# Hybrid attention and SSD block: dt and the sum of the two directions in the mixing matrix, two products per SSD head, the group norm as a replicated row

## Chip, cores and metric

One core of one Trainium2 chip runs the whole layer. The metric is the device time of one execution in microseconds, as a median of three runs: 1584.28 us (1583.84 to 1584.5).

## What is computed

The layer takes 256 tokens of width 2048. It makes one projection of the normed input, attention in 16 heads, a bidirectional Mamba-2 SSD in 32 heads, an output projection and an MLP. The change touches the SSD alone. Cut to it:

```python
dt = softplus(dt_raw + dt_bias)            # (b, S, 2 directions, 8 groups, 4 heads)
y_fwd = ssd_chunked(xs, dt[:, :, 0], A[0], Bm, Cm)          # chunks of 128 tokens
y_bwd = flip(ssd_chunked(flip(xs), flip(dt[:, :, 1]), A[1], flip(Bm), flip(Cm)))
y = y_fwd + y_bwd + xs * d_skip
y = y.reshape(b, S, SSM_W) * silu(z)
y = rms_norm(y.reshape(b, S, 8, 256), norm_g)   # over the 256 channels of a group
```

With a sequence of two chunks, each head's output is x (256 tokens by 64 channels) multiplied by a 256 x 256 matrix over (source token, target token): C.B of the group, times a decay for each direction, times dt of the source token and direction. The forward direction has nothing in the block "source in chunk 2, target in chunk 1", the backward one nothing in the opposite block.

## The kernel before

The program is written by hand, engine by engine, with semaphores. Every weight matrix is streamed from HBM in chunks of 256 rows by 512 columns (SyncE, `load`). ScalarE rounds each chunk to `w_hi` (L478), VectorE makes `w_lo`, what the rounding left (L776), and TensorE does 24 multiplies of 128x256 (or 12 of 128x512) per chunk with high and low parts (`chunk_by_weights`, `chunk_by_tokens`; all matmuls go through the helper line L1178). Time is counted in slots, one chunk each. ScalarE and VectorE prepare the chunk that is four slots ahead (`high_ahead`, `low_ahead`, LEAD = 4); SyncE loads into eight buffers, and a load waits until TensorE has used the chunk eight back.

SSD work is put in between. A window of 24 slots holds the projections of two groups (x, B, C) and of z. A group's own work starts at `GROUP_SLOT` and goes over some 16 slots, k = 0 to 15, a new group every 12 slots. In each slot an engine does first its part for the chunk, then what the group schedule names, in program order, so what waits in a slot holds up the next chunk's part on that engine. On each engine, by k:

- TensorE: k = 0 transposes x and makes C.B for both chunks (`group_products`, psum banks M0 and M1); k = 5 and 7 the products of two heads each into M0, head by head; k = 10 the sums of squares, in two columns for each half of the tokens; k = 11 spreads the root over all partitions, by a multiply of ones with a diagonal.
- VectorE: k = 1 masks C.B into `cbm` (six blocks of 128 x 128) and scales x by dt for each direction into `xdt_f` and `xdt_b` (`scale_x`, L790); k = 2 to 5 `mix_head` (L799) multiplies a head's six decay blocks by `cbm`; the convolution of the next group in pieces (`CONV_SLOTS`), its SiLU at k = 11; k = 8 the skip and gate; k = 9 the low part of the squares; k = 11 the mean (`group_mean`, L845) and the diagonal (L851); k = 12 the norm; k = 14 the low part of the result.
- ScalarE: the next group's decays for one head at each of `DECAY_SLOTS` (k = 6, 7, 8, 10), four Relu of 128 columns, two Exp of 128 and one of 512; the tanh of the next group's convolution at k = 11; k = 9 the square and its high part; k = 12 copies the spread row out of M1 (L539); k = 13 the high part of the result.
- GpSimd: the power of -0.5 on the two means per token half (`norm_root_of`, L437), and the same for Q and K.
- SyncE: loads the decay rows of a group, replicated over the partitions, at slots 2 and 14 (`decay_loads`), behind a wait until the decays of the group before were made.

Of the kernel before, what the change touches and what calls it, by code (L numbers as in the profile page):

```python
# [28 lines left out]
P = 128  # L29
# [5 lines left out]
EPS = 1e-6  # L35
# [15 lines left out]
DECAY_SLOTS = {6: 0, 7: 1, 8: 2, 10: 3}  # L51
CONV_SLOTS = {3: ((0, 0, 4),), 4: ((1, 0, 2),), 5: ((1, 2, 4),), 6: ((2, 0, 4),), 7: ((3, 0, 4),), 9: ((4, 0, 2),),
              10: ((4, 2, 4),)}
# [26 lines left out]
def build(nc, x, norm_mix_g, w_in, q_norm_g, k_norm_g, rel_bias, conv_w, conv_b, dt_bias, a_log,  # L80
# [17 lines left out]
    with ctx:  # L98
# [71 lines left out]
        xdt_f = place("xdt_f", [P, TT, SEQ], at=at_of(lo2, 2048))  # L170
        norm_diag = place("norm_diag", [P, TT, P], at=at_of(lo2, 1024))
        rnorm = place("rnorm", [P, SEQ], at=at_of(lo2, 1024))

        sq_hi = place("sq_hi", [P, 2, SEQ], f32r, at=cat_base + 32768)
        sq_lo = place("sq_lo", [P, 2, SEQ], f32r, at=at_of(lo2, 2048))
        norm_ms, norm_root = small[:, 32:34], small[:, 34:36]
        gate_n = gate_t
        hi1 = [phase + 4096]
        xdt_b = place("xdt_b", [P, TT, SEQ], at=at_of(hi1, 2048))
# [55 lines left out]
        def sem(name):  # L235
# [20 lines left out]
        args_ready, decays_ready, mix_ready, y_done = (sem(n) for n in (  # L256
            "args_ready", "decays_ready", "mix_ready", "y_done"))
        x_transposed, xtok_ready, cb_done, cb_masked = (sem(n) for n in (
            "x_transposed", "xtok_ready", "cb_done", "cb_masked"))
        gated, gate_squared, norm_summed, ms_ready, root_ready, diag_ready, norm_spread, rn_ready = (sem(n) for n in (  # L260
            "gated", "gate_squared", "norm_summed", "ms_ready", "root_ready", "diag_ready", "norm_spread", "rn_ready"))
        normed, ssd_hi, ssd_lo = sem("normed"), sem("ssd_hi"), sem("ssd_lo")
# [28 lines left out]
        def _(sp):  # L291
# [111 lines left out]
        @block.gpsimd  # L403
        def _(pool):
            pool.memset(ident[:, :], 1.0).then_inc(consts, 1)
            pool.memset(ones[:, :], 1.0).then_inc(consts, 1)
            pool.memset(halfneg[:, :], -0.5).then_inc(consts, 1)
            pool.memset(relw[:, :], 1.0).then_inc(consts, 1)
            pool.memset(one_row[:, :], 1.0).then_inc(consts, 1)
            pool.memset(prefix[:, :, 0:1], 0.0).then_inc(consts, 1)  # L410
            pool.memset(conv_in[:, :, :, 0:2], 0.0).then_inc(consts, 1)
            pool.memset(conv_in[:, :, :, SEQ + 2:SEQ + 4], 0.0).then_inc(consts, 1)
            pool.memset(dtcol[:, 3:4], 1.0).then_inc(consts, 1)
            pool.memset(mask[:, :, :], 1.0).then_inc(consts, 1)
# [19 lines left out]
            def norm_root_of(G):  # L434

                pool.wait_ge(ms_ready, G + 1)
                pool.tensor_tensor(norm_root, norm_ms, halfneg[:, 0:2], ALU.pow).then_inc(root_ready, 1)  # L437

            with pool.Fori(1, 4) as w:
                norm_root_of(2 * (w - 1))  # L440
                norm_root_of(2 * (w - 1) + 1)
            for n in range(2):
                norm_root_of(6 + n)
                qk_root(n)
            with pool.Fori(1, 4) as a:
                qk_root(2 * a)
                qk_root(2 * a + 1)


        @block.scalar  # L450
        def _(act):
# [62 lines left out]

            def conv_tanh_of(G):
# [3 lines left out]
            def next_group(G, i, k):  # L519
# [3 lines left out]
                if k == 11:  # L523
                    conv_tanh_of(G)

            def ssd_slot(s, m, more=True):

                for i, o in enumerate(GROUP_SLOT):
                    G, k = 2 * m + i, s - o
                    if not 0 <= k < 16 or (i == 2 and not more):  # L530
                        continue
                    if k == 9:
# [67 lines left out]
            for s in range(CH - LEAD, WIN):  # L600
# [23 lines left out]
                if s == 19:  # L624
                    conv_tanh_of(0)
                if s == 17:
                    act.wait_ge(m1_free, 1)
                if 17 <= s < 21:
                    decays(0, s - 17)
                next_group(1, 1, s - GROUP_SLOT[2])  # L630
# [86 lines left out]
        def _(dve):  # L717
# [66 lines left out]
            def scale_x(G):  # L784

                dve.wait_ge(x_transposed, G + 1)
                for n, (xdt, H) in enumerate(((xdt_f, 4 * G), (xdt_b, 32 + 4 * G))):
                    dt = tokp[:, 3:5, ds(H, PER_GROUP)].rearrange("p t (h o) -> p t h o", o=1)\
                        .broadcast_to([P, TT, PER_GROUP, 64])
                    ins = tt_(xdt[:, :, :].rearrange("p t (h e) -> p t h e", e=64),  # L790
                              M0.rearrange("p (t h e) -> p t h e", t=TT, e=64), dt, ALU.mult)
                ins.then_inc(xtok_ready, 1)

            def mix_head(G, h):
# [4 lines left out]
                tt_(w[:, :, :], w[:, :, :], cbm[:, :, :], ALU.mult).then_inc(mix_ready, 1)  # L799
# [47 lines left out]
            def group_diag(G):  # L847

                dve.wait_ge(root_ready, G + 1)
                for t in range(TT):  # L850
                    ins = ts_(norm_diag[:, t, :], ident[:, :], norm_root[:, t:t + 1], None, ALU.mult)  # L851
                ins.then_inc(diag_ready, 1)
# [35 lines left out]
            def ssd_slot(s, m, more=True):  # L888

                for i, o in enumerate(GROUP_SLOT):  # L890
# [3 lines left out]
                    if k == 1:  # L894
                        mask_cb(G)
                        scale_x(G)
# [8 lines left out]
                    if k == 11:  # L905
                        group_diag(G)
# [148 lines left out]
            for s in range(CH - LEAD, WIN):  # L1055
# [8 lines left out]
                if s == 21:  # L1064
# [4 lines left out]
                    scale_x(0)  # L1069
# [106 lines left out]
        def _(pe):  # L1176
# [62 lines left out]
            def ssd_slot(s, m, more=True):  # L1239
                for i, o in enumerate(GROUP_SLOT):  # L1240
# [5 lines left out]
                    if k in (5, 7):  # L1246
                        pe.wait_ge(xtok_ready, G + 1)
                        pe.wait_ge(mix_ready, 4 * G + k - 3)
                        for h in (k - 5, k - 4):
                            rows, ch = slice(64 * (h % 2), 64 * (h % 2) + 64), slice(64 * h, 64 * h + 64)  # L1250
                            c0 = SEQ * (h // 2)
                            both, second, first = slice(c0, c0 + SEQ), slice(c0 + P, c0 + SEQ), slice(c0, c0 + P)
                            mm(M0[rows, both], xdt_f[:, 0, ch], mix[h][:, 4:6, :], True, False)
                            mm(M0[rows, both], xdt_b[:, 1, ch], mix[h][:, 0:2, :], False, False)
                            mm(M0[rows, second], xdt_f[:, 1, ch], mix[h][:, 2, :], False, False)
                            mm(M0[rows, first], xdt_b[:, 0, ch], mix[h][:, 3, :], False, True).then_inc(y_done, 1)
                    if k == 10:
# [3 lines left out]
                        for t in range(TT):  # L1261
# [3 lines left out]
                    if k == 11:  # L1265
                        pe.wait_ge(diag_ready, G + 1)
                        pe.wait_ge(ms_ready, G + 1)
                        for t in range(TT):
                            ins = mm(M1[:, P * t:P * (t + 1)], ones_r[:, :].bitcast(f32), norm_diag[:, t, :], True, True)
                        ins.then_inc(norm_spread, 1)  # L1270
# [208 lines left out]
```

## Time and profile before

| | us |
|---|---|
| median of the runs | 1584.28 |
| profiled execution | 1584.14 |
| its span, first to last instruction | 1582.40 |
| TensorE matmul busy | 1554.7 (98%) |
| VectorE busy | 944.8 (60%) |
| ScalarE busy | 733.8 (46%) |
| GpSimd busy | 35.0 (2%) |

Busy is the union of an engine's instructions. TensorE's granted clock is at its full level (0.997 as a mean). The SSD groups stand in the first quarter, from about 93 us to 430 us. Of the sections below, the weight load (PEld) runs beside the multiplies. An f32 multiply is recorded as two entries. "x2" behind a row means two instructions merged; times are starts from the begin of the span, then the length.

### The profile page before, as it was taken

How to read it: one execution, taken by the hardware profiler on the slowest of the kernel's cores; microseconds unless marked ns; L12 is line 12 of the kernel's file. 1: busy time of each engine (PE TensorE's matmuls, PEld its weight loads, DVE VectorE, ACT ScalarE, POOL GpSimd, SP SyncE). 2: the span in 40 equal slices, each digit the busy share in tenths (PEclk: the TensorE clock that was granted, in tenths of full speed). 3: DMA queues.
4: the chain of work that ended last, by engine and by line, in shares of the span. 5: the costliest groups of instructions: out<-in, count | busy, mean ns of one | idle time of the engine just before them, and what ended most of it. 6: DMA issues, size and time to landing. Idle time of an engine off the chain costs nothing.

```text
span 1582.4 us, 25561 instructions
## 1 busy us (share of the span) xinstructions
PE 1554.7 (98%) x9693; PEld 1395.8 (88%) x9693; DVE 944.8 (60%) x1226; ACT 733.8 (46%) x1011; POOL 35.0 (2%) x36
## 2 busy tenths in 40 slices
PE   6999999999999999999999999999999999999998
PEld 6999999998888888888889998899988998889987
DVE  5878787778666666665465554364454455435543
ACT  4476556656354544444443443434433344424431
POOL 0000000000100000000000000000000000000000
PEclk9999999999999999999999999999999999999999
DMA  8776666555566656575656655666555665666564
GB/s 233 227 216 175 184 174 174 172 175 154 161 186 175 180 176 178 175 237 180 195 181 182 185 183 192 193 166 183 190 190 171 186 181 192 191 174 183 186 196 136
DMA packets 186324, 291.50 MB, mean 184 GB/s; under 512 B 13533, under 2 KB 67151, under 8 KB 185984
## 3 DMA queue, kind: packets, MB, share of 16 engines
q1 hardware_dynamic: 183748, 285.92, 60.3%
q10 hardware_dynamic: 2492, 4.36, 0.9%
q8 instruction: 64, 1.05, 0.3%
q14 instruction: 20, 0.16, 0.0%
HBM read 288.04 MB, written 5.34 MB: 185 GB/s over the span
## 4 chain that ended last, share of the span: by engine, by line
PE 95%; DMA 2%; DVE 1%; ACT 1%; issue 0%; DVEq 0%; SPq 0%; ACTq 0%
PE psum L1178 94%; DMA raw<-in_w_in 1%; DVE w_lo L776 1%; DMA x_in<-in_x 1%; PE psum L1288 0%; PE psum L1308 0%; PE psum L1221 0%; DMA decay_rows<-prefix 0%; PE psum L1231 0%; ACT w_hi L478 0%; DVE xg L751 0%; ACT mix L507 0%; ACT squares_act L464 0%; DVE actT_lo L771 0%; SPq L298 0%
## 5 line engine op out<-in xcount | busy, mean ns | idle before, releaser
L776 DVE TENSOR_TENSOR w_lo<-raw,w_hi 128x1024 fp32r<-128x1024 f32 x512 | 611.0, 1221 | 165.4 <-ACT w_hi L478 162.0
L478 ACT ACTIVATE w_hi<-raw 128x1024 fp32r<-128x1024 f32 x512 | 527.8, 1053 | 390.0 <-DMA raw<-in_w_down 166.2
L1178 PE MATMUL psum<-actT_lo,w_hi 128*128 128x256 f32 x1792 | 514.1, 287 | 9.6 <-DVE w_lo L776 9.6
L1178 PE MATMUL psum<-actT_hi,w_hi 128*128 128x256 f32 x1792 | 509.5, 284 | 0.0
L1178 PE MATMUL psum<-actT_hi,w_lo 128*128 128x256 f32 x1792 | 509.4, 284 | 0.0
L1178 PEld LDWEIGHTS psum<-actT_lo,w_hi 128*128 128x128 f32 x1792 | 346.3, 193 | 14.4 <-DVE w_lo L776 9.4
L1178 PEld LDWEIGHTS psum<-actT_hi,w_lo 128*128 128x128 f32 x1792 | 346.3, 193 | 0.2
L1178 PEld LDWEIGHTS psum<-actT_hi,w_hi 128*128 128x128 f32 x1792 | 346.3, 193 | 0.0
L1178 PE MATMUL psum<-w_hi,hid_lo 128*128 128x512 f32 x512 | 199.2, 389 | 0.0
L1178 PE MATMUL psum<-w_lo,hid_hi 128*128 128x512 f32 x512 | 199.2, 389 | 0.0
L1178 PE MATMUL psum<-w_hi,hid_hi 128*128 128x512 f32 x512 | 199.2, 389 | 0.0
L1178 PE MATMUL psum<-w_hi,actT_lo 128*128 128x512 f32 x384 | 153.3, 399 | 0.0
L1178 PE MATMUL psum<-w_lo,actT_hi 128*128 128x512 f32 x384 | 150.0, 391 | 0.0
L1178 PE MATMUL psum<-w_hi,actT_hi 128*128 128x512 f32 x384 | 150.0, 391 | 0.0
L1178 PEld LDWEIGHTS psum<-w_hi,hid_hi 128*128 128x128 f32 x512 | 96.1, 188 | 20.1
L1178 PEld LDWEIGHTS psum<-w_hi,hid_lo 128*128 128x128 f32 x512 | 96.1, 188 | 19.9
L1178 PEld LDWEIGHTS psum<-w_lo,hid_hi 128*128 128x128 f32 x512 | 96.1, 188 | 19.6
L1155 DVE SCALAR_TENSOR_TENSOR acc<-psum,inv_ms,acc 128x512 f32<-128x512 f32 x32 | 22.6, 747 | 146.7 <-PE psum L1178 146.7
L1142 DVE TENSOR_TENSOR relu_sq<-relu_t 128x1024 f32<-128x1024 f32 x16 | 19.6, 1226 | 147.1 <-ACT relu_t L696 147.1
L1178 PE MATMUL psum<-w_hi,cat_lo 128*128 128x512 f32 x256 | 100.8, 394 | 0.0
L1178 PE MATMUL psum<-w_hi,cat_hi 128*128 128x512 f32 x256 | 99.8, 390 | 0.0
L1178 PE MATMUL psum<-w_lo,cat_hi 128*128 128x512 f32 x256 | 99.8, 390 | 0.0
(192 smaller groups left out, 1277.7 us busy)
## 6 DMA issues: line engine op xcount, KB each, us to landing
raw<-in_w_in SPq DMA_DIRECT2D x128, 512.0 KB
raw<-in_w_up SPq DMA_DIRECT2D x128, 512.0 KB
raw<-in_w_down SPq DMA_DIRECT2D x128, 512.0 KB
raw<-in_w_out SPq DMA_DIRECT2D x64, 512.0 KB
raw<-in_w_in SPq DMA_DIRECT2D x64, 256.0 KB
raw<-in_w_in SPq DMA_DIRECT2D x128, 128.0 KB
decay<-decay_rows SPq DMA_DIRECT2D x16, 512.0 KB, 5.5
rel_tiles<-rel_rows ACTq DMA_DIRECT2D x1, 3072.0 KB, 19.8
```

What stands on the lines that cost most here:

```text
L478: act.activation(w_hi[j][:, :, :], raw[j][:, :, :], ACT.Copy).then_inc(hi_ready, 1)
L776: tt_(w_lo[j][:, :, :], raw[j][:, :, :], w_hi[j][:, :, :].bitcast(f32), ALU.subtract).then_inc(lo_dve, 1)
L1142: tt_(relu_sq[:, :, :], relu_t[:, :, :], relu_t[:, :, :], ALU.mult).then_inc(relu_squared, 1)
L1155: stt_(acc[:, n, t, :], bank_pair(n)[:, t, :], inv_ms[:, 2, t:t + 1], acc[:, n, t, :], ALU.mult, ALU.add).then_inc(down_added, 1)
L1178: return pe.matmul(o, lhsT, rhs, start=first, stop=last, **kw)
```

## The change

The mixing matrix gets dt and the sum of both directions: `mix_head` multiplies each of a head's six blocks by dt of its source token and direction (a scalar per partition) and by `cbm` in one operation (four instructions for the blocks 0-1, 2, 3, 4-5), and then adds block 2 to block 1 and block 3 to block 4, after a wait for its own products. With it a head has one 256-wide matrix row of blocks for each chunk of source tokens, so TensorE does two products a head (256 columns each), in the order chunk 1 of both heads, chunk 2 of both heads. `scale_x` goes; ScalarE copies x from M0 to `xtok` at k = 1 (`copy_x`).

The norm's sum of squares is made by four multiplies of ones with the squares, 256 columns, so each partition holds the whole row. VectorE takes the mean of it (256 columns, `group_mean`), ScalarE makes Ln and Exp with scale -0.5, and VectorE one Newton step in three dependent instructions ahead of the norm. The diagonal, its multiplies, the copy out of M1 and GpSimd's power for the SSD are gone.

In the schedule, the fourth head's decays go from k = 10 to 12, two pieces of the convolution from 9 and 10 to 8 and 9 (behind the own work of the group in that slot), the tanh from k = 11 to 10, and the decay loads from slots 2 and 14 to 5 and 17.

```diff
-DECAY_SLOTS = {6: 0, 7: 1, 8: 2, 10: 3}
-CONV_SLOTS = {3: ((0, 0, 4),), 4: ((1, 0, 2),), 5: ((1, 2, 4),), 6: ((2, 0, 4),), 7: ((3, 0, 4),), 9: ((4, 0, 2),),
-              10: ((4, 2, 4),)}
+DECAY_SLOTS = {6: 0, 7: 1, 8: 2, 12: 3}
+CONV_SLOTS = {3: ((0, 0, 4),), 4: ((1, 0, 2),), 5: ((1, 2, 4),), 6: ((2, 0, 4),), 7: ((3, 0, 4),), 8: ((4, 0, 2),),
+              9: ((4, 2, 4),)}
...
-                if s == 2 and m is not None:
+                if s == 5 and m is not None:
                     sp.wait_ge(decays_ready, 8 * m + 4)
                     load_decay(2 * m + 1)
-                if s == 14 and m is not None and w is not None:
+                if s == 17 and m is not None and w is not None:
...
+            def copy_x(G):
+                act.wait_ge(x_transposed, G + 1)
+                act.activation(xtok[:, :, :], M0.rearrange("p (t s) -> p t s", t=2), ACT.Copy).then_inc(xtok_ready, 1)
...
-                if k == 11:
+                if k == 10:
                     conv_tanh_of(G)
...
-                    if k == 12:
-                        act.wait_ge(norm_spread, G + 1)
-                        act.activation(rnorm[:, :], M1[:, 0:SEQ], ACT.Copy).then_inc(m1_free, 1)
+                    if k == 11:
+                        act.wait_ge(m1_free, G + 2)
+                        act.activation(log_ms[:, :], mean_sq[:, :], ACT.Ln).then_inc(ln_ready, 1)
+                        act.wait_ge(ln_ready, G + 1)
+                        act.activation(rnorm[:, :], log_ms[:, :], ACT.Exp, scale=-0.5).then_inc(rn_ready, 1)
...
             def mix_head(G, h):
-                tt_(w[:, :, :], w[:, :, :], cbm[:, :, :], ALU.mult).then_inc(mix_ready, 1)
+                for k0, k1, src, col in ((0, 2, 4, 32 + H), (2, 3, 4, H), (3, 4, 3, 32 + H), (4, 6, 3, H)):
+                    ins = stt_(w[:, k0:k1, :], w[:, k0:k1, :], tokp[:, src, ds(col, 1)], cbm[:, k0:k1, :],
+                               ALU.mult, ALU.mult)
+                ins.then_inc(scaled, 1)
+                dve.wait_ge(scaled, H + 1)
+                tt_(w[:, 1:5:3, :], w[:, 1:5:3, :], w[:, 2:4, :], ALU.add).then_inc(mix_ready, 1)
...
             def group_mean(G):
-                ts_(norm_ms, M1[:, 0:2 * TT:2], 1.0 / (4 * 256), EPS, ALU.mult, ALU.add).then_inc(ms_ready, 1)
+                ts_(mean_sq[:, :], M1[:, 0:SEQ], 1.0 / (4 * 256), EPS, ALU.mult, ALU.add).then_inc(m1_free, 1)
             def group_norm(G):
+                dve.wait_ge(rn_ready, G + 1)
+                stt_(newton[:, :], rnorm[:, :], -0.5, rnorm[:, :], ALU.mult, ALU.mult).then_inc(newton_step, 1)
+                dve.wait_ge(newton_step, 3 * G + 1)
+                tt_(newton[:, :], newton[:, :], mean_sq[:, :], ALU.mult).then_inc(newton_step, 1)
+                dve.wait_ge(newton_step, 3 * G + 2)
+                stt_(rnorm[:, :], newton[:, :], 1.5, rnorm[:, :], ALU.add, ALU.mult).then_inc(newton_step, 1)
+                dve.wait_ge(newton_step, 3 * G + 3)
...
-                            mm(M0[rows, both], xdt_f[:, 0, ch], mix[h][:, 4:6, :], True, False)
-                            mm(M0[rows, both], xdt_b[:, 1, ch], mix[h][:, 0:2, :], False, False)
-                            mm(M0[rows, second], xdt_f[:, 1, ch], mix[h][:, 2, :], False, False)
-                            mm(M0[rows, first], xdt_b[:, 0, ch], mix[h][:, 3, :], False, True).then_inc(y_done, 1)
+                        for t in range(TT):
+                            for h in (k - 5, k - 4):
+                                ins = mm(M0[64 * (h % 2):64 * (h % 2) + 64, SEQ * (h // 2):SEQ * (h // 2 + 1)],
+                                         xtok[:, t, 64 * h:64 * h + 64], mix[h][:, 4 - 4 * t:6 - 4 * t, :],
+                                         t == 0, t == TT - 1)
...
-                        for t in range(TT):
-                            for n, (sq, c) in enumerate(((sq_lo, 0), (sq_lo, 1), (sq_hi, 0), (sq_hi, 1))):
-                                ins = mm(M1[:, 2 * t:2 * t + 2], sq[:, c, P * t:P * t + P], ones_r[:, 0:2], n == 0, n == 3)
+                        for c in range(2):
+                            mm(M1[:, 0:SEQ], ones_r[:, :], sq_lo[:, c, :], c == 0, False)
+                            ins = mm(M1[:, 0:SEQ], ones_r[:, :], sq_hi[:, c, :], False, c == 1)
```

## Rows read from the trace of the kernel before

**Rows 1.** The page: TensorE's busy time, and shares of the chain by engine.

```profile
PE 1554.7 (98%) x9693; PEld 1395.8 (88%) x9693; DVE 944.8 (60%) x1226; ACT 733.8 (46%) x1011; POOL 35.0 (2%) x36
...
PE 95%; DMA 2%; DVE 1%; ACT 1%; issue 0%; DVEq 0%; SPq 0%; ACTq 0%
```

**Rows 2.** Windows: length, busy of PE, PEld, DVE, ACT, POOL; clock, DMA share, GB/s.

```profile
220.04:262.32 42.28, 42.28 (x343) 40.46 (x342) 32.72 (x51) 26.38 (x49) 1.64 (x1) 1.00 0.60 172
...
346.88:388.00 41.12, 41.12 (x235) 34.62 (x234) 33.73 (x52) 25.35 (x48) 1.61 (x1) 1.00 0.53 154
```

**Rows 3.** Timeline of TensorE across a pair of heads (start, length, what).

```profile
235.03 0.28 PE L1178 MATMUL psum<-actT_hi,w_lo 128*128 128x256 f32 x1
235.15 0.28 PE L1178 MATMUL psum<-actT_hi,w_hi 128*128 128x256 f32 x1
235.36 0.43 PE L1178 MATMUL psum<-mix,xdt_f 128*64 128x256 f32 x1
...
236.28 0.43 PE L1178 MATMUL psum<-mix,xdt_f 128*64 128x256 f32 x2
...
236.55 0.38 PE L1178 MATMUL psum<-mix,xdt_f 128*64 128x256 f32 x1
236.60 0.27 PE L1178 MATMUL psum<-mix,xdt_b 128*64 128x128 f32 x1
...
237.95 0.28 PE L1178 MATMUL psum<-actT_hi,w_lo 128*128 128x256 f32 x1
```

**Rows 4.** Timeline of TensorE at the norm's two steps of a group.

```profile
254.78 0.28 PE L1178 MATMUL psum<-ones_r,sq_lo 128*128 128x2 f32 x2
...
255.79 0.28 PE L1178 MATMUL psum<-actT_hi,w_lo 128*128 128x256 f32 x1
...
258.55 0.61 PE L1178 MATMUL psum<-norm_diag,ones_r 128*128 128x128 f32 x4
...
259.11 0.28 PE L1178 MATMUL psum<-actT_hi,w_lo 128*128 128x256 f32 x1
```

**Rows 5.** VectorE: timeline (first three), groups by shape (busy us, mean ns, idle before).

```profile
233.25 0.95 DVE L799 TENSOR_TENSOR mix<-mix,cbm 128x768 f32<-128x768 f32 x1
234.12 0.88 DVE L816 SCALAR_TENSOR_TENSOR conv<-conv_in,parA,conv 128x256 f32<-128x256 f32 x2
...
255.77 0.16 DVE L845 TENSOR_SCALAR small<-psum 128x2 f32<-128x2 f32 x1 [2.01 <-PE psum L1178]
...
L816 DVE SCALAR_TENSOR_TENSOR conv<-conv_in,parA,conv 128x256 f32<-128x256 f32 x96 | 40.7, 478 | 0.0
L799 DVE TENSOR_TENSOR mix<-mix,cbm 128x768 f32<-128x768 f32 x32 | 30.4, 951 | 0.0
L1155 DVE SCALAR_TENSOR_TENSOR acc<-psum,inv_ms,acc 128x512 f32<-128x512 f32 x32 | 22.6, 747 | 146.7 <-PE psum L1178 146.7
...
L944 DVE TENSOR_TENSOR qkT_lo<-psum,qkT_hi 128x256 fp32r<-128x256 f32 x16 | 6.6, 415 | 0.0
```

**Rows 6.** ScalarE: groups by shape (first two), then its timeline.

```profile
L539 ACT ACTIVATE rnorm<-psum 128x256 f32<-128x256 f32 x8 | 3.1, 385 | 22.1 <-PE psum L1178 22.1
...
L454 ACT ACT_TABLE_LOAD x1 | 1.3, 1283 | 1.3 <-PEq L1466 1.3
...
251.61 1.27 ACT L507 ACTIVATE mix<-decay,tokn 128x128 f32<-128x128 f32 x4
...
253.88 1.05 ACT L478 ACTIVATE w_hi<-raw 128x1024 fp32r<-128x1024 f32 x1
```

**Rows 7.** Group 0: SyncE's wait (total, times, longest), timelines of VectorE and TensorE.

```profile
SPq L326 <- ACT mix L513: 8.5, 1, 8.5
...
105.66 1.22 DVE L776 TENSOR_TENSOR w_lo<-raw,w_hi 128x1024 fp32r<-128x1024 f32 x1 [2.63 <-ACT w_hi L478]
...
125.22 0.69 DVE L903 TENSOR_TENSOR sq_lo<-gate_sq,sq_hi 128x512 fp32r<-128x512 f32 x1 [0.23 <-ACT sq_hi L536]
...
127.94 0.28 PE L1178 MATMUL psum<-ones_r,sq_lo 128*128 128x2 f32 x2
```

More of the change, by code:

```diff
@@ L169, in build @@
         gate_sq = place("gate_sq", [P, 2, SEQ], at=at_of(lo2, 2048))
-        xdt_f = place("xdt_f", [P, TT, SEQ], at=at_of(lo2, 2048))
-        norm_diag = place("norm_diag", [P, TT, P], at=at_of(lo2, 1024))
+        xtok = place("xtok", [P, TT, SEQ], at=at_of(lo2, 2048))
+        mean_sq = place("mean_sq", [P, SEQ], at=at_of(lo2, 1024))
+        log_ms = place("log_ms", [P, SEQ], at=at_of(lo2, 1024))
         rnorm = place("rnorm", [P, SEQ], at=at_of(lo2, 1024))
+        newton = place("newton", [P, SEQ], at=at_of(lo2, 1024))
         sq_hi = place("sq_hi", [P, 2, SEQ], f32r, at=cat_base + 32768)
-        sq_lo = place("sq_lo", [P, 2, SEQ], f32r, at=at_of(lo2, 2048))
-        norm_ms, norm_root = small[:, 32:34], small[:, 34:36]
+        sq_lo = place("sq_lo", [P, 2, SEQ], f32r, at=lo2[0] - 3072)
         gate_n = gate_t
         hi1 = [phase + 4096]
-        xdt_b = place("xdt_b", [P, TT, SEQ], at=at_of(hi1, 2048))
         mask = place("mask", [P, 5, P], at=at_of(hi1, 2560))
@@ L255, in build @@
         decay_in = sem("decay_in")
-        args_ready, decays_ready, mix_ready, y_done = (sem(n) for n in (
-            "args_ready", "decays_ready", "mix_ready", "y_done"))
+        args_ready, decays_ready, scaled, mix_ready, y_done = (sem(n) for n in (
+            "args_ready", "decays_ready", "scaled", "mix_ready", "y_done"))
         x_transposed, xtok_ready, cb_done, cb_masked = (sem(n) for n in (
             "x_transposed", "xtok_ready", "cb_done", "cb_masked"))
-        gated, gate_squared, norm_summed, ms_ready, root_ready, diag_ready, norm_spread, rn_ready = (sem(n) for n in (
-            "gated", "gate_squared", "norm_summed", "ms_ready", "root_ready", "diag_ready", "norm_spread", "rn_ready"))
-        normed, ssd_hi, ssd_lo = sem("normed"), sem("ssd_hi"), sem("ssd_lo")
+        gated, gate_squared, norm_summed, ln_ready, rn_ready, newton_step, normed, ssd_hi, ssd_lo = (sem(n) for n in (
+            "gated", "gate_squared", "norm_summed", "ln_ready", "rn_ready", "newton_step", "normed", "ssd_hi", "ssd_lo"))
         z_tanh, z_ready = sem("z_tanh"), sem("z_ready")
@@ L432, in qk_root, with att_window @@
                 pool.tensor_tensor(qk_s[:, 2, :], qk_s[:, 1, :], halfneg[:, :], ALU.pow).then_inc(qk_rs, 1)
[L434 to L445, printed above, removed]
+            def att_window(a):
                 qk_root(2 * a)
                 qk_root(2 * a + 1)
+            att_window(0)
+            with pool.Fori(1, 4) as a:
+                att_window(a)
         @block.scalar
@@ L531, in ssd_slot @@
                         continue
+                    if k == 1:
+                        copy_x(G)
                     if k == 9:
@@ L623, in _ @@
                     xbc_copy(1, 1, 0)
-                if s == 19:
+                if s == 18:
                     conv_tanh_of(0)
@@ L629, in _ @@
                     decays(0, s - 17)
+                if s == 21:
+                    copy_x(0)
                 next_group(1, 1, s - GROUP_SLOT[2])
@@ L781, in low_ahead @@
                 low(U0 + n, j)
[L784 to L792, printed above, removed]
             def mix_head(G, h):
@@ L895, in ssd_slot @@
                         mask_cb(G)
-                        scale_x(G)
                     if 2 <= k < 6:
@@ L904, in ssd_slot @@
                             .then_inc(sq_low, 1)
-                    if k == 11:
-                        group_diag(G)
                     if k == 12:
@@ L1068, in _ @@
                     mask_cb(0)
-                    scale_x(0)
                 if s > 21:
@@ L1248, in ssd_slot @@
                         pe.wait_ge(mix_ready, 4 * G + k - 3)
[L1249 to L1252, printed above, removed]
-                            mm(M0[rows, both], xdt_f[:, 0, ch], mix[h][:, 4:6, :], True, False)
-                            mm(M0[rows, both], xdt_b[:, 1, ch], mix[h][:, 0:2, :], False, False)
-                            mm(M0[rows, second], xdt_f[:, 1, ch], mix[h][:, 2, :], False, False)
-                            mm(M0[rows, first], xdt_b[:, 0, ch], mix[h][:, 3, :], False, True).then_inc(y_done, 1)
+                        for t in range(TT):
[3 more added lines that the diff above has]
+                                         t == 0, t == TT - 1)
+                                if t == TT - 1:
+                                    ins.then_inc(y_done, 1)
                     if k == 10:
@@ L1260, in ssd_slot @@
                         pe.wait_ge(cb_masked, G + 1)
-                        for t in range(TT):
-                            for n, (sq, c) in enumerate(((sq_lo, 0), (sq_lo, 1), (sq_hi, 0), (sq_hi, 1))):
-                                ins = mm(M1[:, 2 * t:2 * t + 2], sq[:, c, P * t:P * t + P], ones_r[:, 0:2], n == 0, n == 3)
+                        for c in range(2):
+                            mm(M1[:, 0:SEQ], ones_r[:, :], sq_lo[:, c, :], c == 0, False)
+                            ins = mm(M1[:, 0:SEQ], ones_r[:, :], sq_hi[:, c, :], False, c == 1)
                         ins.then_inc(norm_summed, 1)
[L1265 to L1270, printed above, removed]
             def att_slot(s, g):
```

4 lines of the change are left out of this document (removed).

## Prediction

> **What bounds the kernel now.** I read the busy line and the chain of waits first, then sums by stretch, then engine timelines of one SSD group, then the costs by shape. TensorE is busy 98% of the span and carries 95% of the chain [rows 1]. In the stretches of one SSD group (12 chunks of 24 projection multiplies, 42.28 us) it is busy all 42.28 us; VectorE is busy 32.72 us (some 1.1 more in even groups, where the SiLU of z falls, 1024 columns), ScalarE 26.38 [rows 2]. So until another engine becomes the pacer, TensorE time taken out of a group comes out of the total one for one. There are 8 groups; number 6 runs at 41.12 us [rows 2].
>
> **TensorE, the products.** A projection multiply starts 0.12 us after the last (235.03, 235.15), so two steps are 0.24. Across the products of one pair of heads, from the last multiply before (235.15) to the second after (237.95), it takes 2.80: net 2.56 us a pair [rows 3]. Each f32 product is recorded as two passes; head one's first starts at 235.36. Head two's first pass starts at 236.28 and its second at 236.55, while head one's last is still to start at 236.60 [rows 3]: the two heads write different halves of the partitions and do run at once. Backwards from 237.95: head two has four passes of 256 columns and four of 128. I take 0.27 us for the first (236.28 to 236.55), three at 0.215 and four at half of that, the rate at which one pass would use 512 clocks; they end at 237.62, so the exit is 0.33, and the entry (235.15 to 235.36) 0.21.
> After the change a pair is two products a head, all of 256 columns, the heads in turn: four passes a head. If they overlap wholly: 0.21 + 0.27 + 3 x 0.215 + 0.33 - 0.24 = 1.22, a gain of 1.34 a pair, 21.5 us for 16. If nothing overlaps, eight passes: 0.21 + 0.27 + 7 x 0.215 + 0.33 - 0.24 = 2.08, a gain of 0.48, 7.7 in all. I take overlap, because head two was seen to start four passes ahead of head one's end.
> The Trainium skill ("TensorE: Matmul & The Clock Gate", Part 3 on packing small matmuls) says that multiplies keep program order in start and end. The row above shows a later one started first, so it does not hold here to the letter. By that rule head two would trail by one pass, 0.215 us a pair, and TensorE's gain would be 18 us instead of 21.5.
>
> **TensorE, the norm.** The eight two-column multiplies take 254.78 to 255.79 less one step: 0.89 us; the spreading of the diagonal 258.55 to 259.11 less one step: 0.44 [rows 4]. Four multiplies of 256 columns in the rounded type take their place, shape and type of the projections: 0.48. Gain 0.85 a group, 6.8 in all.
> TensorE alone: 2 x 1.34 + 0.85 = 3.53 a group, 28.3 us in all, a group of 38.75 us (group 6: 37.6). Without overlap 1.81 a group, 14.5 in all, a group of 40.47.
>
> **VectorE.** An instruction occupies it for its duration less 0.09 (the mix of 0.95 at 233.25, the next at 234.12 [rows 5]). By shape [rows 5]: scalar-tensor-tensor of 256 columns 0.48, of 512 0.75, so 128 columns about 0.34; tensor-tensor of 256 columns 0.415, of 768 0.95, so 512 columns 0.68; a w_lo of 1024 columns 1.22 [rows 7]. What I give for other lengths is from these slopes, about 1.05 us per 1000 columns. A dependent instruction waits for the full duration plus some 0.03.
> Per head: now 0.86. After: 2 x 0.39 + 2 x 0.25, the last one's 0.09 back, 0.03, and the sum 0.33: 1.75; +0.9, or 3.6 a group. Rows of before bound the four shapes tightly (0.25 to 0.39 each for the short ones: up to +1.1 a group). The scaling of x goes: 2 x 0.59 = -1.2. The mean becomes 256 columns: +0.3. The diagonal goes: -0.4. The three dependent Newton steps: 0.51 + 0.45 + 0.51 = +1.5. Sum +3.8 a group. As occupancies a group without the z part is then: 12 w_lo x 1.13 = 13.6, four heads 7.0, convolution 7.7 (4 x 0.33 and 16 x 0.40), mask 0.9, silu 1.1, gate 1.5, low parts 0.6 + 0.8, mean 0.35, Newton and norm 2.1: 35.7; with z 36.8. Against 38.75 that fits only if VectorE hardly waits.
>
> **ScalarE.** Added: the copy of x (512 columns, 0.55), and Ln and Exp of 256 columns (0.39 each [rows 6]) for the copy of the row. The trace has a single table load, 1.28 us [rows 6], for Square, Copy, Relu, Exp and Tanh together. Whether Ln shares these tables it doesn't show: nothing, or a load out and one back in every group, 2.6 us. I take two loads: every function that is used now has already had its place under the one load, and Ln is the only new one. The Trainium skill ("ScalarE: Activation LUTs", on table sets) lists Exp with Tanh in one set and Ln in another.
> The loads fall between the mean and the row's reciprocal root. The POOL work and its wait go (0.6 us idle, off the path).
>
> **The loop VectorE - ScalarE - VectorE.** Let VectorE's mean start at 0. ScalarE has just done the conv's tanh and splits chunk 15 until 0.95; VectorE's w_lo of it ends at 2.1 (0.6 idle), silu at 3.2. ScalarE: load, Ln, load, Exp (1.28 + 0.39 + 1.28 + 0.39): row at 4.3, the split of chunk 16 at 5.3 (1.05 less 0.09 [rows 6]). VectorE idles 2.1 until it; w_lo, Newton, norm: 8.5. ScalarE makes a head's decays (2.27, from 251.61 to 253.88 [rows 6]) and splits chunk 17 at 8.5; w_lo 9.7, mask 10.6. The next split comes after cat_hi, the copy of x and, in odd groups, the conv's copy: at 11.0 or 11.9, again 0.4 or 1.3 idle. From there VectorE has all it needs to the end of its list: 38.9, with z (even) 40.0, with the conv's copy (odd) 39.8. Today 2.0 us of idle stand at that mean alone [rows 5], which is the room that this uses up.
> So a group is about 39.9 us, paced by this loop, TensorE waiting 1.15 us each for the low part of the squares (it needs it after the chunk of slot 10). Groups 1 to 5: 5.75. Group 6, where TensorE would run at 37.6: 2.4. Group 7 has no next group to prepare and its VectorE has room: 0.
> Group 0: today the squares' low part ends at 125.8 and TensorE wants it at 127.94 [rows 7]. With 3.6 for the heads and 0.8 for the two convolution pieces moved ahead of it, it would be at 130.2, TensorE (2.7 earlier) at 125.3. But x is not scaled (-1.2), and the 8.5 us wait of SyncE for the decays [rows 7], behind which the weight loads stood and VectorE idle for 2.63 us, goes as the load is issued three slots later: about 125.9 to 126.4. I put 0.6 us on it. The later decay loads still land well ahead (5 slots of some 3 us before use): nothing.
> Sum: 28.3 - 5.75 - 2.4 - 0.6 = 19.5 us. The profiled execution took 1584.14 (span 1582.40 and 1.7 around it), the median of the runs is 1584.28. Forecast 1564.8.
>
> **Rivals.**
> (a) The products don't overlap. For: the new order has not run, and overlap was seen only at the seam of two heads. Against: that seam. TensorE then gains 14.5; at 40.47 it paces itself, but for 0.7 in group 6: 1570.5.
> (b) Ln costs no loads, or they stand beside other work. The loop is 2.6 shorter, 37.4, and TensorE stays the only bound: 28.3 - 0.6: 1556.6.
> (c) A table switch costs more than its row. The one load has 1.3 us of idle before it [rows 6]; if that were part of it, 2.6 each, the loop is 42.5: 5 x 3.75 + 4.9 + 0.6 = 24.2 lost, 1580.2. The Trainium skill ("ScalarE: Activation LUTs", on what a table load costs) adds a drain and gives 2.66 us a switch: by it 1581. Against: the row puts that idle time to another engine's sequencer, at the program's start; there was then nothing to drain, so it weighs little either way.
> (d) Slower: the same loop on ScalarE, between Ln and Exp, becomes longer than the gain. With c the group, TensorE's gain is gone at 0.6 + 5(c - 38.75) + (c - 37.6) = 28.3, c = 43.2, a switch of 2.9 us. At 3.5 us: c = 44.3, 1591.
> (e) The sum of the directions is one wait longer, or the short shapes cost as the long ones: +1 to +2 us a group on the loop, 1571 to 1576.
>
> **Numbers.** Forecast (1561 to 1569) 0.5; (b) 0.18; (a) and (e) 0.23; (c) 0.05; (d) 0.03; nothing of it 0.01. The range 1556 to 1574 leaves out about 0.15. 0.2% is 3.2 us, what a measurement here can tell from no change: faster (below 1581.1) 0.94, same 0.03, slower 0.03.
>
> **What would show it.** TensorE in turn: pairs' starts overlapping, 1.5 us from the last multiply before to the second after (2.3 if not). Multiplies of ones with the squares at 0.12. Two loads of 1.28 us a group, VectorE idle about 2 us before w_lo of chunk 16. Groups of about 39.9 us with a TensorE wait of some 1 us for sq_lo. VectorE busy about 36.5 to 37.6 a group. The forecast is wrong if there is no TensorE wait in the groups (then b), or if the loads are not there or longer.

## The result, and the profile after

| | before | after |
|---|---|---|
| median, us (lowest to highest) | 1584.06 (1583.76 to 1584.5) | 1574.49 (1573.56 to 1575.52) |
| profiled execution, its span | 1584.14, 1582.40 | 1575.52, 1573.80 |

The ratio is 0.994, with an interval of 0.9922 to 0.9957: faster by 9.6 us, where 19.5 were forecast, and 0.5 us outside the range. The page of the changed kernel, its busy line and its chain by engine, against [rows 1]:

```profile
PE 1532.7 (97%) x9501; PEld 1375.0 (87%) x9501; DVE 969.9 (62%) x1346; ACT 761.7 (48%) x1043; POOL 22.9 (1%) x28
...
PE 79%; DVE 9%; issue 5%; ACT 4%; DMA 2%; DVEq 1%; ACTq 0%; SPq 0%
```

TensorE has lost 16 points of the chain: 8 to VectorE, 3 to ScalarE, as forecast, and 5 to "issue", in which an engine waits for nothing that the profile shows. The share alone says little: most of these 74 us are pauses of less than 0.3 us or some 1 us long between dependent instructions, and e1 below, 9 us faster, still has 79% and 4%. What needs an explanation is the one long piece among them, 3.73 us. The windows of groups 0 to 5 of the changed kernel, each from the transposes of a group to those of the next (columns as in [rows 2], which has 42.28 for each):

```profile
93.99:132.90 38.91, 38.91 (x317) 37.40 (x317) 34.15 (x61) 28.00 (x50) 0.00 (x0) 1.00 0.66 186
...
132.90:172.94 40.04, 38.96 (x319) 37.34 (x317) 35.76 (x66) 29.76 (x53) 0.00 (x0) 1.00 0.62 185
172.94:217.21 44.27, 40.57 (x318) 38.45 (x317) 37.02 (x67) 28.97 (x52) 0.00 (x0) 0.96 0.59 167
217.21:257.26 40.05, 38.97 (x319) 37.34 (x317) 35.75 (x66) 29.77 (x53) 0.00 (x0) 1.00 0.61 184
257.26:302.17 44.91, 40.52 (x318) 38.83 (x317) 37.64 (x68) 30.43 (x55) 0.00 (x0) 0.96 0.58 164
302.17:340.88 38.71, 38.71 (x318) 37.28 (x317) 35.14 (x66) 28.56 (x50) 0.00 (x0) 1.00 0.63 190
```

Groups 1 and 3 are the forecast's 39.9. Groups 2 and 4 are 4.4 and 5.0 longer, at a lower clock, and the last row gives 1.2 back. VectorE's timeline where group 2 and group 4 go wrong (the bracket is the idle before an instruction and what ended it), and the piece of the chain of waits at the first of them (start, length, what; DVEq is VectorE's sequencer, L1087 the line of its loop over the SSD windows):

```profile
191.51 1.23 DVE L778 TENSOR_TENSOR w_lo<-raw,w_hi 128x1024 fp32r<-128x1024 f32 x1 [3.86 <-issue]
...
274.99 1.23 DVE L778 TENSOR_TENSOR w_lo<-raw,w_hi 128x1024 fp32r<-128x1024 f32 x1 [3.02 <-issue]
```

```profile
186.95 0.70 DVE conv L809 x2
187.66 3.73 issue
191.38 0.08 DVEq L1087
```

The trace has the loop's COMPARE_BRANCH at 186.88 and at 271.20; the sequencer's next instruction follows 4.50 and 3.67 us later, and before the change 0.33 and 0.31 us later. Two things went up with it: VectorE's recorded instructions in one turn of the loop (two SSD groups), from 251 and 255 to 320, and the packets of the instruction queue q14, from 20 to 32 in the whole execution. From 95 to 345 us, first before and then after the change:

```profile
q14 instruction: 4, 0.03, 0.0%
...
q14 instruction: 14, 0.11, 0.2%
```

The packets' times point at the jumps. The kernel before has none from 149 to 373 us, over both of its jumps; the changed kernel has them at 189.34, 192.39 and 196.46 behind the first jump, at 273.03, 275.59 and 280.14 behind the second, and six more elsewhere in that stretch. So the theory: the body had become too long to be still at hand at the jump back, and VectorE waits until it is fetched. The Trainium skill ("Runtime: NRT & Kernel Launch", on instruction fetch mechanics) has this mechanism: a taken branch whose target isn't in the window at hand forces a fetch by DMA. Its window of 512 instructions for engines other than TensorE is larger than any turn recorded here, so its size alone doesn't tell when the fetch begins. The section also says that the window is two blocks of 256, of which the next is fetched while the current one runs; how much of it lies behind the jump, no run here shows.

TensorE then waits. Its table of waits (for what, us in total, times, the longest), all those of over 2 us:

```profile
PE psum L1311 <- DMA rowsB<-in_k_norm_g: 10.7, 1, 10.7
PE psum L1171 <- DVE w_lo L778: 9.6, 4, 2.7
PE psum L1171 <- DVE sq_lo L899: 7.9, 5, 2.6
PE psum L1171 <- DVE mix L796: 4.4, 2, 2.6
```

The first two rows are of before too. The wait for sq_lo was forecast at some 8.8 in all; the one for the mix is the late VectorE. And something follows the longest ones. TensorE in group 2, at the products after such a wait:

```profile
198.34 1.60 PE L1171 MATMUL psum<-mix,xtok 128*64 128x256 f32 x8 [2.60 <-DVE mix L796]
...
200.47 0.41 PE L1171 MATMUL psum<-actT_hi,w_hi 128*128 128x256 f32 x1
200.68 0.41 PE L1171 MATMUL psum<-actT_lo,w_hi 128*128 128x256 f32 x1
```

and the windows from there, and from the end of the wait of 2.62 us for sq_lo in group 4:

```profile
198.34:201.90 3.56, 3.56 (x17) 2.61 (x18) 3.56 (x6) 1.83 (x7) 0.00 (x0) 0.56 0.18 50
294.35:297.80 3.45, 3.45 (x16) 3.45 (x17) 2.85 (x5) 2.66 (x3) 0.00 (x0) 0.51 0.17 50
```

The granted clock is at the lower of its two levels (1.2 instead of 2.4 GHz) for 3.4 us, multiplies follow each other by 0.21 instead of 0.12 us, and each time some 1.7 us more are lost (half of the 3.4). Group 2 by these rows: 2.60 and 1.7 = 4.3 beyond its usual wait; group 4: 1.76 + 2.62 + 1.7 - 1.1 = 5.0.

### The profile page after: what moved, and what is told of

Its sections match the earlier page's. It is cut to its first block, busy times and chain, and to the rows that moved or that the text cites. A ratio compares the mean times of both kernels' runs of the same rounds, so it can differ in the third digit from the quotient of the medians.

```text
span 1573.8 us, 25410 instructions
## 1 busy us (share of the span) xinstructions
PE 1532.7 (97%) x9501; PEld 1375.0 (87%) x9501; DVE 969.9 (62%) x1346; ACT 761.7 (48%) x1043; POOL 22.9 (1%) x28
## 4 chain that ended last, share of the span: by engine, by line
PE 79%; DVE 9%; issue 5%; ACT 4%; DMA 2%; DVEq 1%; ACTq 0%; SPq 0%
PE psum L1171 77%; DVE w_lo L778 2%; DVE mix L792 2%; DVE conv L813 2%; ACT w_hi L470 1%; DMA raw<-in_w_in 1%; DMA x_in<-in_x 1%; PE psum L1275 0%; PE psum L1295 0%; PE psum L1214 0%; ACT mix L499 0%; ACT L537 0%; ACT conv_t L513 0%; DVE gate_t L832 0%; DMA decay_rows<-prefix 0%
```

## The experiments

Fourteen kernels were run, each timed beside the kernel before on the same chip. VectorE's "jump" is the time from the COMPARE_BRANCH to its sequencer's next instruction, first and second turn.

| kernel | median, us | ratio (interval) | a group, us | turn; jump |
|---|---|---|---|---|
| changed | 1574.49 | 0.994 (0.9922 to 0.9957) | 40.04, 44.27, 40.05, 44.91, 38.71 | 320; 4.50, 3.67 |
| e1: loop written out | 1565.54 | 0.9879 (0.9863 to 0.9896) | 40.03, 40.24 | none |
| e2: no Ln | 1563.91 | 0.9866 (0.985 to 0.9883) | 38.71, 44.44, 38.71, 42.31 | 320; 6.10, 4.91 |
| e3: both | 1557.38 | 0.9829 (0.9812 to 0.9845) | 38.71 | none |
| e4: e3, head by head | 1556.77 | 0.9824 (0.9807 to 0.984) | 38.73 | none |
| e5: new mix, old norm | 1575.11 | 0.9945 (0.9928 to 0.9962) | 39.56, 43.23, 39.56, 46.81 | 310; 5.37, 6.63 |
| e6: e5, loop written out | 1564.39 | 0.9878 (0.9861 to 0.9894) | 39.56 | none |
| e7: old mix, new norm | 1582.01 | 0.998 (0.997 to 0.9989) | 41.43 | 264; 0.33, 0.31 |
| e8: before, 72 more a turn | 1583.99 | 1.0 (0.999 to 1.0009) | 42.28 | 326, 322; 2.87, 3.08 |
| e9: before, loop written out | 1584.2 | 1.0004 (0.9994 to 1.0013) | 42.28 | none |
| e10: e1, tanh at slot 19 | 1566.44 | 0.989 (0.9873 to 0.9906) | 40.05, 40.26 | none |
| e11: e10, no Newton step | 1564.45 | 0.9878 (0.9861 to 0.9894) | 39.65, 39.89 | none |
| e12: before, 24 more a turn | 1585.21 (one run) | | 42.28 | 278, 275; 0.33, 0.31 |
| e13: e1, decays at k = 14 | 1566.21 | 0.9885 (0.9868 to 0.9901) | 40.03, 40.24 | none |
| e14: e13, no Newton step | 1557.65 | 0.9827 (0.9811 to 0.9844) | 38.71, 38.82 | none |

**The fetch.** e1 writes VectorE's loop out; e9 does the same to the kernel before.

```diff
-            with dve.Fori(1, 4) as w:
+            for w in range(1, 4):
```

> The changed kernel, but VectorE's loop over the three SSD windows is written out (no jump back; the other engines keep their loops). Theory A: the 3.86 and 3.02 us of idle after the loop's two jumps on VectorE (187.66 and 271.97 us in the changed kernel's trace), which nothing in the profile explains, is the fetch of the loop's code; in its wake TensorE stalls and its clock falls. Then both stretches without work on VectorE are gone, groups 2 and 4 take 40.0 us as groups 1 and 3 do (44.3 and 44.9 now), group 5 goes from 38.7 to about 40, TensorE's granted clock stays full in the SSD part: 7 to 8 us less, about 1567. Theory B: the idle belongs to something else at that place (a weight load that is late, a wait): 1574 to 1575 as now.

Two windows of e1, groups 1 and 2:

```profile
132.39:172.42 40.03, 38.96 (x318) 37.34 (x317) 35.73 (x66) 29.76 (x53) 0.00 (x0) 1.00 0.63 184
172.42:212.66 40.24, 38.96 (x318) 37.33 (x317) 36.86 (x67) 28.95 (x52) 0.00 (x0) 1.00 0.66 183
```

The long groups are gone, the low clock in the SSD part with them, q14 is at 22 packets, and the time is 1565.5: 1.5 us below what was expected of this run, and 0.7 above the 1564.8 of the prediction.

> The kernel before, with VectorE's loop over the SSD windows written out. Control for the written-out loop alone. Theory (the loss of the change is the fetch after VectorE's jump, and the turn of the loop before, 251 to 255 recorded instructions, is short enough not to need it): no fetch to take away, so 1584 us within 1.5. Rival (writing the loop out saves something of its own, register arithmetic or branches, and the 9 us it gave on the changed kernel are not the fetch): 1575 to 1580.

Nothing changed: writing the loop out gives nothing where there is no fetch. e8 and e12 lengthen the turn of the kernel before (`dve.sem_inc(filler, 1)`, three or one in each slot).

> The kernel before, its VectorE loop over the SSD windows made longer by 72 semaphore increments that nothing waits for (from some 255 recorded instructions a turn to some 327, the changed kernel has 320). Theory A, the loop's length against the instruction buffer: idle of 3 to 5 us without a releaser on VectorE behind each of the two jumps and instruction packets on queue 14 there, neither of which the kernel before has. VectorE has some 8 us of idle a group to take it up, so the time changes little: 1584 to 1588. Theory B (the idle comes from what the new instructions do, not from their number): no such idle; 1584 to 1585.

> The kernel before with one more semaphore instruction in each slot of VectorE's loop, 24 a turn, so about 275 to 279 recorded instructions a turn (264 jumped without delay, 310 with 5.4 us, 322 to 326 with 2.9 us until VectorE's next sequencer instruction). One look, to narrow where the fetch starts. If the limit is some 256 plus what the engine has already passed on, the delay after the jump is there; if it lies nearer to 310, the next sequencer instruction follows within 0.4 us. The time stays at 1584 in both cases, since the loop's VectorE has 2.7 us of other work behind the jump.

With 322 to 326 instructions q14 rises to 31 packets and the jump takes 2.9 us, though nothing of the change is in this kernel; with 278 it takes 0.33. q14 has 11 packets from 150 to 350 us in e8, as in the changed kernel, and none in e12 and e7. So the fetch begins between 278 and 310 recorded instructions a turn, and more instructions alone make it. Whether the length of the turn decides, or where the jump falls in the whole stream, was not separated: the first jump is the 409th to 434th recorded VectorE instruction in the runs without a fetch, the 476th to 486th in those with one. But e8 lost no time. Its VectorE around the jump at 183.81:

```profile
183.12 1.22 DVE L777 TENSOR_TENSOR w_lo<-raw,w_hi 128x1024 fp32r<-128x1024 f32 x1
184.25 0.95 DVE L800 TENSOR_TENSOR mix<-mix,cbm 128x768 f32<-128x768 f32 x1
185.12 1.38 DVE L813 TENSOR_SCALAR conv<-conv_in,parA,parB 128x256 f32<-128x256 f32 x4
186.81 1.23 DVE L777 TENSOR_TENSOR w_lo<-raw,w_hi 128x1024 fp32r<-128x1024 f32 x1 [0.30 <-issue]
```

Its sequencer had passed 2.7 us of work to the engine ahead of the gap, so VectorE stood for 0.30 us only; the changed kernel had 0.8 us there, and its groups had no slack for the rest.

**One half of the change alone.** e5 has the new mixing and products and keeps the old norm, e7 the reverse; e6 is e5 with the loop written out.

> The kernel before with only the first half of the change: dt and the sum of the directions in mix_head, two products a head with the heads in turn, x copied by ScalarE, and the schedule's moves. The norm is the old one. TensorE should save 2.68 us a group (39.6), VectorE's loop has neither the table loads nor the Newton steps and is below that, the idle after the jumps is absorbed in part. If so 20 to 21 us less than before, 1563 to 1565. If VectorE's extra 3.6 us a group are alone too much: about 40 to 41 us a group, 1568 to 1574.

> The mixing half of the change alone on the kernel before, with VectorE's SSD windows written out. If code fetch after the jump took its gain (1575.1 with the loop, groups of 43.2 and 46.8 us among four of 39.6), all groups from 1 to 5 are 39.6 and the time is 1563 to 1565. If it was something else, 1573 to 1576.

> The other half alone: the changed kernel with the old scaling of x, the old mix_head and the four products a head. TensorE saves 0.85 us a group (41.4); the loop of VectorE and ScalarE with its two table loads is some 37.5 and doesn't pace it: 6 to 7 us less than before, about 1577.5. If the table loads or the Newton steps are late for TensorE by themselves: no gain, 1580 to 1585.

e5 missed its expectation for the reason that e1 names: a turn of 310. e6 has TensorE busy in all of its 39.56 us a group; that it is as fast as e1 (1564.39 against 1565.54) says what the new norm is worth beside the new mix: nothing. e7's group, 41.43, is the 42.28 - 0.85 of the forecast, to the hundredth. At the start of the second MLP quarter its profiled execution was 6.1 us ahead of the one before, as expected, but 1.5 us at the end: its waits for w_lo at the ends of MLP quarters are up to 4.0 us long instead of 2.7, in a part that the change doesn't touch, and the granted clock is at its lower level for 6.8 us around the last of them (0.50 from 1393.62 to 1400.45). Its ten runs go from 1578.19 to 1583.91, so much of this is the spread of executions; why their median is only 2.9 us below that of before stays open.

**The table loads.** e2, e3 and e4 make a Copy in the place of Ln, so their root is not the norm's.

```diff
-                        act.activation(log_ms[:, :], mean_sq[:, :], ACT.Ln).then_inc(ln_ready, 1)
+                        act.activation(log_ms[:, :], mean_sq[:, :], ACT.Copy).then_inc(ln_ready, 1)
```

> The changed kernel with Copy in place of Ln, so that ScalarE needs no other table (the root's value is then another one). Theory A: the 16 table loads (20.5 us on ScalarE) stand in the loop VectorE - ScalarE - VectorE that paces a group; without them the loop is some 2.5 us shorter, about 37.5, below TensorE's 38.8. Groups 1 and 3 at 38.8, groups 2 and 4 still with the idle after the jump but absorbed in part (about 41), group 6 about 38: 10 to 12 us less, about 1563. Theory B: the loads lie beside other work and VectorE's own length paces the group: no more than 2 us less, 1572 to 1574.

> The changed kernel with VectorE's SSD windows written out and Copy in place of Ln (so no table loads; the root's value is another one). If the table loads and the jump's fetch are all that keeps the TensorE saving back, every group from 1 to 5 takes 38.7 to 38.85 us and group 6 about 37.5, with no TensorE wait after group 0: 1557 (8 us less than with the windows written out alone). If VectorE's own length still paces: 39 us or more a group, 1560 to 1563.

e3's windows show TensorE without a wait, at 38.72 us; the forecast had 38.75 for TensorE alone:

```profile
131.50:170.22 38.72, 38.72 (x319) 37.29 (x318) 36.30 (x69) 28.02 (x52) 0.00 (x0) 1.00 0.62 189
```

**The order of the heads.** e4 is e3 with the loops over t and h exchanged: both products of one head, then both of the other.

> As e3_unroll_noloads, but the four products of a pair head by head (both products of head one, then both of head two). TensorE paces here, so its cost shows in full. If the gain of the alternation is that two heads' passes run at once, and head by head only part of them can: between nothing and full overlap lost, which is up to 0.86 us a pair, 1.7 a group: groups of 39.2 to 40.5 us, 1561 to 1571. The passes before the change suggest that the second head can still start some passes early, so I expect the lower half of it, about 1564. If the order doesn't matter: groups of 38.8, 1557.

Missed: no difference. TensorE at one pair of heads in the changed kernel, and then in e4 (eight recorded passes merged in a row):

```profile
188.51 0.28 PE L1171 MATMUL psum<-actT_hi,w_hi 128*128 128x256 f32 x1
188.71 1.08 PE L1171 MATMUL psum<-mix,xtok 128*64 128x256 f32 x8
189.73 0.39 PE L1171 MATMUL psum<-actT_lo,w_hi 128*128 128x256 f32 x1
189.95 0.28 PE L1171 MATMUL psum<-actT_hi,w_lo 128*128 128x256 f32 x1
```

```profile
148.41 0.28 PE L1171 MATMUL psum<-actT_hi,w_hi 128*128 128x256 f32 x1
148.62 1.09 PE L1171 MATMUL psum<-mix,xtok 128*64 128x256 f32 x8
149.64 0.39 PE L1171 MATMUL psum<-actT_lo,w_hi 128*128 128x256 f32 x1
```

Eight passes in 1.08 us in either order: the engine runs two heads at once when four passes of one stand ahead of the other's as well. In the changed kernel the passes start two at a time, 0.01 us apart (188.71 and 188.72, then 188.98 and 188.99), and so they do in e4. The gain of the products comes from two f32 products a head instead of four, not from the turns.

**The start.** e10 puts the tanh of group 0 back from slot 18 to slot 19 of the first window; in the changed kernel its first transposes come 1.3 us later than before.

> The changed kernel with VectorE's loop written out and the tanh of group 0 put back to slot 19 of the first window. Theory for the start: the tanh in slot 18 stands ahead of a head's decays and a chunk's split on ScalarE and holds up the first transposes by some 1.3 us; put back, group 0 starts near 92.7 us and the time falls from 1565.5 to about 1564.2. Rival: the later tanh makes the convolution's SiLU of group 0 later by as much, and nothing is gained: 1565.5.

The rival was right: the transposes come 1.0 us earlier than in e1 (92.53 against 93.57), and group 0 is 1.0 us longer (39.80 against 38.82). What sets group 1's start is VectorE's list, not the transposes.

**What sets the 40.03.** With the fetch gone e1 is still 8 us above e3. e11, which is e10 otherwise, leaves out the Newton step (three VectorE instructions; the root's last digits are less exact), e13 moves the fourth head's decays on ScalarE, and e14 does both.

```diff
-DECAY_SLOTS = {6: 0, 7: 1, 8: 2, 12: 3}
+DECAY_SLOTS = {6: 0, 7: 1, 8: 2, 14: 3}
...
-                if s == 5 and m is not None:
+                if s == 7 and m is not None:
...
-                if s == 17 and m is not None and w is not None:
+                if s == 19 and m is not None and w is not None:
```

> As the one with the tanh put back, and VectorE's Newton step on the replicated root left out (the root is used as ScalarE makes it, so its last digits are less exact). Theory (VectorE's three dependent instructions stand in the loop VectorE - ScalarE - VectorE that paces a group at 40.03 us): the loop loses 1.3 to 1.5 us, a group falls to TensorE's own 38.7 us, group 6 to 37.5 or a little over: 5 x 1.3 + 1.2 to 2 = 7.7 to 8.5 less, about 1556 us, with the two table loads still there. Rival (the loop is set by the table loads and the decays that ScalarE queues behind, and the Newton step stands beside them): a group stays at 39.5 to 40.0 and the time at 1562 to 1564.

> The changed kernel with VectorE's loop written out, the fourth head's decays at k = 14 instead of 12 on ScalarE, and the decay loads at slots 7 and 19. Theory (both branches of the loop end at once, 8.5 us after the mean: ScalarE with decays and split of chunk 17, VectorE with the Newton step and the norm): only the idle behind them goes, 0.44 and 1.35 us in turn, so a group of 39.1 to 39.6 us and 1558 to 1562 us. Rival 1 (the decays alone pace the loop): TensorE's own 38.7 us and 1557. Rival 2 (the decays beside, or their work costs the same two slots later): 40.0 and 1565.5.

> The same with VectorE's Newton step left out as well (the root's last digits less exact). Theory: both branches are now short, TensorE paces the groups itself at 38.7 us with both table loads in every group, group 6 at 37.5 to 38: 1556 to 1558 us, and no wait of TensorE for the squares' low part above 0.3 us. Rival (the two table loads stand in the loop whatever is around them): a group of 39.3 us or more, 1560 us or more.

Out of 1.3 us, e11 won 0.4 a group against e10: VectorE now stood before the low part of chunk 17 for a split that ScalarE made only after the decays.

```profile
171.87 1.22 DVE L778 TENSOR_TENSOR w_lo<-raw,w_hi 128x1024 fp32r<-128x1024 f32 x1 [2.05 <-ACT w_hi L470]
173.01 0.68 DVE L848 TENSOR_TENSOR gate_t<-gate,rnorm 128x512 f32<-128x512 f32 x1
175.09 1.23 DVE L778 TENSOR_TENSOR w_lo<-raw,w_hi 128x1024 fp32r<-128x1024 f32 x1 [1.40 <-ACT w_hi L470]
```

In group 6 it lost 1.2 again (41.21 against 39.99 in e10): after a wait of 1.83 us the granted clock was at 0.50 from 364.02 to 367.43. e13 won nothing: now ScalarE stood for VectorE, which was at the Newton step and the norm.

```profile
171.93 1.99 ACT L470 ACTIVATE w_hi<-raw 128x1024 fp32r<-128x1024 f32 x2
176.44 0.91 ACT L543 ACTIVATE cat_hi<-gate_t,parB 128x256 f32 x2 [2.53 <-DVE gate_t L855]
```

Only the two together (e14) bring the group to TensorE's own time, with both table loads still in it:

```profile
132.06:170.77 38.71, 38.71 (x318) 37.28 (x317) 34.38 (x63) 29.70 (x53) 0.00 (x0) 1.00 0.63 188
```

e14, at 1557.65 us, is the fastest of these that still makes the norm, if with a less exact root: 0.9827 of the time before. e3's 1557.38 has no loads at all, so with both branches short the loads cost nothing. Group 6 missed its expectation by a little: 38.5 us, with a wait of 0.76 for sq_lo. Of the three theories only e14's held. The forecast's own working had both branches end 8.5 us after the mean; I had read that as a reason to expect a gain from each, and it says the opposite.

## Why the prediction was wrong

By its own steps, from the span of 1562.9 that it implies to the 1573.8 measured, 10.9 us:

- **TensorE, the products: right.** 1.22 us a pair were forecast with overlap. From the last multiply before to the second after it is 188.51 to 189.95, 1.44, less 0.24 = 1.20. The reason given, a seam of two heads, was right and the order in turn not needed (e4). By the rule of order of the Trainium skill ("TensorE: Matmul & The Clock Gate", Part 3 on packing small matmuls), as it was weighed in the prediction, the group would have been 0.43 us longer, which e3's 38.72 excludes.
- **TensorE, the norm: right.** e7's 0.85 a group; the four multiplies of ones follow each other by 0.12.
- **TensorE alone 38.75 a group:** 38.71 to 38.72 in e3 and e14.
- **Two loads of 1.28 us: right**, and nothing on top. ScalarE at the mean of group 1 in the changed kernel:

```profile
168.35 1.04 ACT L470 ACTIVATE w_hi<-raw 128x1024 fp32r<-128x1024 f32 x1
169.40 1.28 ACT L537 ACT_TABLE_LOAD   x1
170.70 0.42 ACT L537 ACTIVATE log_ms<-mean_sq 128x256 f32<-128x256 f32 x1
171.13 1.28 ACT L539 ACT_TABLE_LOAD   x1
172.43 0.42 ACT L539 ACTIVATE rnorm<-log_ms 128x256 f32<-128x256 f32 x1
```

  The first load starts as the split ahead of it ends, and Ln 0.02 us after the load, so no drain stands on either side. The Trainium skill ("ScalarE: Activation LUTs", What ACT_TABLE_LOAD costs) gives 1283 ns, as measured here, and 1380 ns of drain on top, which these rows don't show. Rivals (b) and (c) fall.
- **The loop of 39.9 us: right in size**, 40.04 and 40.05 here, 40.03 and 40.24 in e1. VectorE's idle before chunk 16 is 2.05 (forecast 2.1), and its shapes are within 0.02 us: 344 and 478 ns for the mix, 425 for the sum. Group 6: 39.82 where 40.0 was forecast, 0.2 back. Groups 1 and 3 cost 0.3 together.
- **Group 0: 0.6 forecast.** Group 1 starts at 132.90, against 135.02 before: 2.1 gained, not 2.9. That is 0.8, of which e1 (132.39) has 0.3; the rest differs from run to run (131.50 in e3, 132.84 in e4).
- **The step that failed: VectorE's instructions were counted as occupancy only.** The forecast had each at its duration, and the sequencer at nothing. What it left out is that some 65 more instructions in each turn of the loop put the jump back over a limit. It costs 4.4 us in group 2 and 5.0 in group 4, less the 1.2 back in group 5, 8.2 in all, about 3.4 of it through the clock (twice 1.7) and the rest through TensorE's waits. The medians of e1 and the changed kernel are 9.0 us apart, but not all of that is the fetch: of the 9.3 us between their profiled executions 7.3 lie in groups 1 to 6 (247.80 against 240.48), 0.5 in the start and 1.5 in the last quarters. No rival held this mechanism: (e) has the size, 1571 to 1576, for another reason, and e1 excludes it.
- **The last quarters**, not forecast: from the start of the second MLP quarter to the end, the kernel before, then the changed one:

```profile
1031.19:1582.40 551.21, 541.40 (x3456) 495.45 (x3456) 267.57 (x239) 213.15 (x209) 0.00 (x0) 0.99 0.59 180
```

```profile
1021.05:1573.80 552.75, 542.92 (x3456) 496.92 (x3456) 267.65 (x239) 213.44 (x209) 0.00 (x0) 0.99 0.60 180
```

  1.5 us more for the same work. At the ends of MLP quarters TensorE waits up to 2.7 us for w_lo in both, and the clock fell after all three such waits in the changed execution and after two in the one before. e1 has 551.25, so this is an execution's luck, not the change.

Sum: 8.2 + 0.8 + 0.3 - 0.2 + 1.5 = 10.6 of 10.9. Of the rest, 0.1 lies between group 7 and the second MLP quarter (643.74 us before, 640.35 after: 3.4 gained, where 3.5 was forecast), and 0.1 in group 6, which begins and ends at its transposes with 41.03 before, not with the 41.12 of the forecast.

## What to carry to other kernels

When a change adds instructions to an engine's loop, count them per turn, the register and semaphore instructions too, and look at what the engine has queued at the jump back: a long "issue" idle behind a loop's line (not the share of "issue" in the chain), and packets of the instruction queue there, are the signs, and writing the loop out is the test and the cure. Where a ledger has two branches ending at the same moment, neither is worth shortening alone; find both and move both. And a wait of the engine that paces can cost more than its length, when the clock falls with it: twice 1.7 us here.

## What the runs showed of the hardware that was not expected

- VectorE's jump back: 0.31 to 0.33 us with turns of 251 to 278 recorded instructions, 2.87 to 6.63 us with 310 to 326. SyncE's, with 258 a turn in the MLP, takes 0.28 and 0.26 us. What makes one fetch 2.87 and another 6.63 us stays open. At the loop's last pass through the branch, which isn't taken, the changed kernel has 0.14 us.
- In the changed kernel the granted clock fell to its lower level for 3.4 us at TensorE's waits of 2.60 and 2.62 us, and not at those of 1.76 and 2.04 us; nor did it at the 2.19 us of e1's group 6. But the length of the wait doesn't decide it: the clock fell at waits of 1.83 us (e11, group 6) and 1.86 us (e2, at 288.40), and not at 2.63 us (e5, at 207.12) nor at 2.73 us (the kernel before, at 1398.58). What does was not tried.
- f32 products on two halves of the output partitions overlap also when they are issued head by head: eight passes in 1.09 us (e4).
